# A hybrid decoder layer without the filler matmuls between the output mix and the first expert's up projection

## What is computed

```python
xp = layer_norm(ALPHA * xp + merged @ w_out, ln1_g, ln1_b)   # the "mix" is merged @ w_out

logits = xt @ w_router + b_router
top_v, top_i = lax.top_k(logits, 4)
gate = softmax(top_v)
# tokens are sorted by expert into blocks; for each block of one expert e:
h = xblk @ w_up[e] + b_up[e]
glu, lin = h[:, :1024], h[:, 1024:]
act = min(glu, 7) * sigmoid(1.702 * min(glu, 7)) * (clip(lin, -7, 7) + 1)
y = act @ w_down[e] + b_down[e]          # weighted by gate, added to its tokens

xp = layer_norm(ALPHA * xp + y, ln2_g, ln2_b)
```

## Time and profile before

| | |
|---|---|
| median of 3 runs | 1238.23 us (1238.17 to 1241.14) |
| the profiled execution | 1238.63 us |
| its span, first to last instruction | 1236.8 us |
| PE busy | 1204.3 us, 97% |
| weight loads on PE | 584.1 us, 47% |
| VectorE busy | 373.0 us, 30% |
| ScalarE busy | 195.9 us, 16% |
| read from HBM | 449.69 MB, 366 GB/s over the span |
| mean granted clock of TensorE | 0.996 |

### The profile page before, as it was taken

The page is one execution under the profiler, slowest core; times in us unless marked ns, Lnnn a source line. Parts: engine busy times, 40 slices in busy tenths (PEclk is TensorE's granted clock), DMA queues, the critical chain, the costliest instruction groups (busy, mean ns, idle before and its releaser), DMA issues.

```text
span 1236.8 us, 14949 instructions
## 1 busy us (share of the span) xinstructions
PE 1204.3 (97%) x6439; PEld 584.1 (47%) x6439; DVE 373.0 (30%) x840; ACT 195.9 (16%) x421; POOL 4.6 (0%) x12
## 2 busy tenths in 40 slices
PE   9999999999999999999999999999999999999996
PEld 8888888867333433333333333333333333333332
DVE  1467166135322222222222232222222222222223
ACT  1244472001111000011111001110100100000002
POOL 0000000000000000000000000000000000000000
PEclk9999999999999999999999999999999999999999
DMA  9722455972999999999999999999999999999994
GB/s 369 246 101 90 170 205 185 324 274 84 372 419 428 430 431 429 431 430 431 429 430 429 431 430 430 431 431 430 429 430 432 430 430 430 432 431 429 429 430 168
DMA packets 55553, 451.99 MB, mean 365 GB/s; under 512 B 5808, under 2 KB 24432, under 8 KB 27944
## 3 DMA queue, kind: packets, MB, share of 16 engines
q1 hardware_dynamic: 54784, 448.59, 87.5%
q0 software_dynamic: 272, 1.37, 0.3%
q10 hardware_dynamic: 432, 1.08, 0.2%
HBM read 449.69 MB, written 2.45 MB: 366 GB/s over the span
## 4 chain that ended last, share of the span: by engine, by line
PE 76%; DMA 23%; DVE 1%; issue 0%; ACT 0%; SPq 0%; DVEq 0%
PE pair L1173 24%; PE pair L1218 14%; PE pair L941 13%; DMA slots<-in_w_up 12%; DMA raw<-in_w_up 10%; PE pair L1005 5%; PE pair L1120 4%; PE pair L1246 3%; PE pair L1026 2%; PE pair L1134 1%; PE pair L1203 1%; PE pair L1161 1%; PE pair L1149 1%; PE pair L936 1%; PE pair L918 1%; PE pair L889 1%
## 5 line engine op out<-in xcount | busy, mean ns | idle before, releaser
L1173 PE MATMUL pair<-slots,xg 128*64 128x512 f32 x1424 | 320.2, 595 | 11.4 <-DMA slots<-in_w_up 11.1
L1173 PEld LDWEIGHTS pair<-slots,xg 128*64 128x64 f32 x1424 | 98.4, 137 | 212.9 <-issue 187.4
L1688 DVE TENSOR_TENSOR xT<-xT,pair 128x528 f32<-128x528 f32 x120 | 76.5, 698 | 395.5 <-PE pair L1246 395.5
L1218 PE MATMUL pair<-slots,at 128*64 128x512 f32 x736 | 167.9, 598 | 0.8 <-ACT at L809 0.8
L941 PE MATMUL pair<-xT,raw 128*128 128x264 f32 x704 | 159.6, 386 | 0.0
L1173 PE MATMUL pair<-raw,xg 128*64 128x512 f32 x624 | 141.1, 595 | 8.4 <-DMA raw<-in_w_up 8.4
L941 PEld LDWEIGHTS pair<-xT,raw 128*128 128x128 f32 x704 | 132.7, 190 | 22.7 <-issue 0.4
L805 ACT ACTIVATE sig<-gsb 128x512 f32<-128x512 f32 x32 | 20.1, 630 | 466.0 <-DVE gsb L1698 466.0
L1218 PEld LDWEIGHTS pair<-slots,at 128*64 128x64 f32 x736 | 48.9, 136 | 92.5 <-issue 80.2
L1173 PEld LDWEIGHTS pair<-raw,xg 128*64 128x64 f32 x624 | 43.1, 137 | 97.1 <-issue 80.3
L1246 PE MATMUL pair<-gt,ysb 64*128 64x264 f32 x496 | 69.5, 409 | 0.0
(11 more groups left out here) (284 smaller groups left out, 833.2 us busy)
## 6 DMA issues: line engine op xcount, KB each, us to landing
slots<-in_w_up SPq DMA_DIRECT2D x89, 2048.0 KB, 29.0
slots<-in_w_down SPq DMA_DIRECT2D x44, 2048.0 KB, 33.3
raw<-in_w_up SPq DMA_DIRECT2D x39, 2048.0 KB, 34.9
raw<-in_w_down SPq DMA_DIRECT2D x18, 2048.0 KB, 37.0
raw<-in_w_tiled SPq DMA_DIRECT2D x22, 1024.0 KB, 5.2
raw<-in_w_rnn_out SPq DMA_DIRECT2D x8, 640.0 KB, 11.4
raw<-in_w_attn_out SPq DMA_DIRECT2D x4, 1024.0 KB, 5.1
raw<-in_w_out SPq DMA_DIRECT2D x4, 1024.0 KB, 4.8
```

The source lines that it names most:

```text
L1173: last = pe.matmul(to[h * CAP:(h + 1) * CAP, :], xg[:, 2 * (i % 2) + row, i // 2, :], w[:, c:c + 512], start=False, stop=i == UPP - 1 and ...
L1218: last = pe.matmul(DOWN[h * CAP:(h + 1) * CAP, :], at[:, kk, i - UPP, :], w[:, kk * D + h * 512:kk * D + (h + 1) * 512], start=i == UPP an ...
L1688: ins = dve.tensor_tensor(y, y, more, ALU.add)
```

## The change

Four calls of `stay_busy` go; nothing else is touched. The call at the start of the kernel stays.

```diff
@@ -1075,12 +1075,10 @@
             rank_after(1, 2, True)
             rank_after(1, 0, False).then_inc(ranked, 1)
-            stay_busy(8)
             pe.wait_ge(x1_ready, 3)
             turn_x1(2)
             pe.wait_ge(x1_ready, 4)
             turn_x1(3)
-            stay_busy(2)
             logits(1, 0, KD // 2, 4)
             logits(1, KD // 2, KD, 5)
@@ -1289,7 +1286,6 @@
             gather_tile(1, False, True).then_inc(gathered, 1)
-            stay_busy(3)
             turn_gathered(begin)
             turn_routes()
             run(begin, first_routes)
```

## The result

Without the fillers the kernel is slower: 1245.01 us, the median of 6 runs (1244.27 to 1246.51), against 1239.40 us for the kernel before, the median of 6 (1238.17 to 1241.14). The ratio is 1.0048, with a 95% interval from 1.0037 to 1.0060. That is 5.6 us, outside the range that ends at 1243.0. The second rival's difference was the same (5.6 us, 0.45%), though its time, 1243.8, is lower. The profiled execution took 1246.43 us with a span of 1244.6. The mean granted clock was 0.989 or 0.990 in all six runs; the profiled execution of the kernel before had 0.996.

What follows compares the result with a forecast made beforehand. The weight stream, restarted by the first up projection, was taken to bound the end. Rank +1.0, last fillers -0.1 and possible second fall +0.9 gave +1.8 us: median 1238.23 to 1240.0 us, range 1236.5 to 1243.0.

Steps and rivals of the forecast that it cites:

- The second rival: From rank into first up projection: clock stays low, all pieces longer; 5.6 us, 1243.8 us, 0.45% slower; chance 0.15.
- What bounds the kernel: Second half waits for the weight stream; a delay of the first up projection moves release at 330.23 and end one-for-one.
- The starting point: Kernel before: median of three runs, 1238.23 us, to which the forecast change was added.
- The fall: Clock drop in routing, before or at the logits, some 3 us sooner than the 309.4 us of the trace before.
- logits: Routing logits at half clock: time doubles, adding 1.71 us, since weight loads take 322 ns against 192.
- The rival in which loads keep their pace: At the logits: weight loads not slowed by half clock, logits end at 308.1; 0.5 us, 1238.7 us; chance 0.05.
- The step that failed: Bias rows and hot gather up to the rank: partly half clock, +1.0 us; later durations unchanged, less 0.1.
- the bound of 1.4: At the rank: latest start 313.54 against 312.13 us, with bias rows and gather both at half clock.
- possible second fall: Between 312.8 and 316.8 us, clock may drop again, costing 0 or 1.7 us in the up projection; 0.9 taken.
- the return: Clock back at full in the gather's last part, ahead of the rank; +1.0 us taken there.
- The direct gain: Fillers' removal in routing: 0.15 before logits, 1.15 before rank, 0.1 before gathered rows' turn; 1.4 us saved.
- just in this stretch: In routing, 309.4 to 312.8 us: clock at 0.50, while the slices grant nine tenths or more everywhere.

Runs made afterwards that it cites:

- the delay at full clock: Kernel before with 24 more fillers ahead of the turn of the gathered rows, 27 for 3: 1243.31 us, ratio 1.0032.
- 0, 2, 2, 3: Kernel before without the 8 fillers ahead of the last token tile's turn; those ahead of logits, rank and gathered rows' turn stay: 1241.20 us, ratio 1.0016.
- the last 3 alone: Kernel before with only the 3 fillers ahead of the turn of the gathered rows kept: 1243.40 us, ratio 1.0026.
- turns for the 8: Kernel before with 14 turns of the matrix of ones in place of the 8 fillers ahead of the last token tile's turn: 1239.71 us, ratio 1.0006.
- the thirteen executions: One profiled execution each of the kernels before and after and of eleven follow-up measurements; spans from 1235.5 to 1244.6 us.
- 8, 0, 0, 3: Kernel before without the 2 fillers ahead of the logits and the 2 ahead of the rank: 1238.87 us, ratio 0.9993.
- 8, 0, 0, 0: Kernel before with only the 8 fillers ahead of the last token tile's turn kept: 1242.38 us, ratio 1.0019.
- 8, 2, 0, 1 with bias rows: Kernel before without the 2 fillers ahead of the rank; second bias-row group moved behind the second gather, replacing 2 of the last 3: 1241.09 us, ratio 1.0005.
- 9, 4, 0, 0: Kernel before with 9 fillers ahead of the turn, 4 ahead of the logits and none behind: 1238.94 us, ratio 1.0008.

## Why the prediction was wrong

**What bounds the kernel** was read rightly. The release moved by what the up projection lost, the stream stood still for 7.3 us, and the end followed; the delay at full clock did the same without any change of the clock.

**The starting point** was low. The measured median is 5.0 us above the forecast of 1240.0. Of this 1.2 us lie in the kernel before, whose median is 1239.40 in six runs and was 1238.23 in the three that the forecast began from; the other 3.8 are the change itself, 5.6 us measured for 1.8.

**The fall** came ahead of the logits, as expected, but some 5 us sooner than before and not 3, at the end of the empty pause. The **logits** doubled: 3.45 us measured, 3.42 in the sum. Their weight loads took 330 ns, close to the 322 of the earlier trace rows from which the doubling was argued:

```profile
L1041 PEld LDWEIGHTS pair<-wr,xT 128*128 128x128 f32 x16 | 3.5, 330 | 0.2 <-ACT xT L662 0.2
```

At full clock such a load takes 192 ns. The rival in which loads keep their pace fell. The Trainium skill's page "TensorE: Matmul & The Clock Gate", section "LDWEIGHTS (loading the stationary operand)", gives a load's time by its columns alone, at 1.2 GHz, without a term for the granted clock; the 330 ns disagree with it.

**The step that failed** is the one from the bias rows on. The sum took +1.0 us at the rank, "the gather's last part at full clock again", then "from the rank on I leave the durations as they are", and 0.9 for a possible second fall. There was no return and no second fall but one low stretch of 20 us. The rank began 1.84 us late, above the bound of 1.4; the bound put it at 313.54, and of the 0.43 us beyond 0.33 are the logits' start (306.71 where 306.38 was taken, since the turns ahead of them ran at half clock too, 1.97 us), 0.03 the logits and 0.17 the gather (1.91, where the 1.74 of the earlier trace rows had been in part at full clock), less 0.10 for the bias rows. From the rank to the up projection the rank, bias rows, second gather, turn and route turns took 0.30, 0.69, 0.92, 0.55 and 0.45 us more, less 0.18 for the last fillers, 2.72 in all (by the starts; the pieces add to 2.73), where the forecast had -0.1. Two pieces of before that the earlier trace rows leaves out go into this, the last fillers and the route turns:

```profile
314.63 0.86 PE pair L863 x6
...
316.07 0.76 PE pair L1093 x6
```

In the up projection it was 1.69, where it had 0.9, the mean of 0 and 1.7. That makes 6.25 us against 1.8.

The evidence for the return was one row of one execution, the clock behind 312.8 us in the trace of before (columns as in the earlier trace rows):

```profile
312.80:316.20 3.40, 3.40 (x24) 1.61 (x16) 2.19 (x13) 0.69 (x2) 0.00 (x0) 1.00 0.99 424
```

In that execution two fillers stood in the low stretch, and the argument took them away and kept the return. The experiments show how far the return depends on fillers: with 0, 2, 2, 3 it came after about 3 us, with the last 3 alone after 17, with none after 20. Which filler brings it isn't shown.

**The direct gain** of the fillers' removal was mis-sized too. The 1.15 us ahead of the rank was the pair's time at half clock; at full clock it takes 0.64 (in the trace with turns). Where the clock stays at 1.00, the up projection begins 10.50 us behind the start of the last turn with all groups (turns for the 8), 10.23 without the pair ahead of the rank, 10.23 without the last 3 too, 10.06 with the 8 alone: 0.27 + 0.00 + 0.17 = 0.44 us, not 1.4. Without the pair ahead of the rank the rank waits for VectorE's mask instead; without the pair ahead of the logits these begin sooner, but take 1.99 us for 1.72.

**The second rival** had the mechanism, with a chance of 0.15: the clock was not back at the rank, and every piece from there into the up projection was longer. Its 5.6 us were 6.25 at the release; that the medians differ by just 5.6 is in part luck. Its reason, that every one of the fillers stood in a hole that is now empty, does not hold: in the trace of after PE waits in two places only, 2.2 us ahead of the turn and 0.7 us ahead of the turn of the gathered rows. Between them it is never idle, and the clock stays low all the same. The prediction's "just in this stretch" was not quite so either: the clock is also at 0.50 in the kernel's last few us, where PE has no work left.

**What stays open.** The profiled execution's first DMA piece on the chain is 6.47 us later, the last 7.80, with the release at 6.25. The 1.55 us beyond the release lie within the 1.9 us by which the time behind it differs among the thirteen executions, and runs of one kernel at 0.996 or more differ by up to 3 us (those of before: 1237.0 to 1240.0). Where in the stream that spread comes from isn't shown. Why an execution with the same instructions keeps the clock once and loses it another time isn't shown either, only that the fillers shift how often and for how long it is lost.

## What to carry to other kernels

A filler that costs nothing on its engine's path may still hold something up: ask of each what the clock does in the stretch behind it when the engine pauses, and price the case in which the clock does not come back before the next dense stage. Where one profile shows the clock falling and returning, take it as one draw; the mean clock of each run, beside its time, gives a rough count of how often each course is taken. Here, where the transfers are the bound afterwards, a few microseconds ahead of the first use of the weight ring reached the end, 900 us later, about one for one.

## What the runs showed of the hardware

Once the clock had fallen with no fillers, it stayed at 0.50 for 19.9 us although PE had matmuls or turns in flight for 19.15 of them, and came back in the up projection; with three fillers ahead of that it was back about 3 us sooner (321.6 against 324.6 us). A fall also came with PE at work without a break for 3 us and more ahead of it: in the kernel before at 309.4 us, for 3.4 us, and with 8, 0, 0, 3 at 307.8 us, for 10 us. Turns of 0.12 us each (14 in 1.72 us) in the pause held the clock as the filler matmuls did (seven of ten runs at 0.996 or more, the profiled one at 1.00 throughout). In the second half too the clock fell in three of thirteen traces behind waits for weights: with 8, 0, 0, 0 PE had work for 3.78 of 6.20 us from 1114.0, and from 1120.2 to 1123.6 the mean clock was 0.54. And with some sets of fillers (8, 0, 0, 0; 8, 2, 0, 1 with bias rows; 9, 4, 0, 0) the runs of one kernel fall into two groups some 4 to 5 us apart, 1238 and 1242 to 1243 us, which the mean clock tells apart.
